# Attention in halves of a query tile: scores of 192 keys on quarter-array tiles, and the older half of the values on two row halves

## Chip, cores, metric

One NeuronCore of a Trainium2 chip runs the whole kernel in one launch. The metric is the device time in microseconds, from the start of the program to its end; lower is better.

## What is computed

One layer (DEPTH is 1) of a hybrid decoder block on x of 2048 tokens by 1024 channels, in float32: an adaptive RMSNorm; one projection to 2048 columns; three mixers side by side (a gated linear recurrence HGRN2 of 4 heads, a causal average pooling of 4 groups, and sliding-window attention); an output projection; a second norm; and a gated MLP of 2816 with a causal convolution of width 3. The change touches the attention:

```python
WINDOW = 128                       # 8 query heads, 2 key/value heads, 64 channels each
s = einsum('bnqhgd,bnkhd->bnhgqk', qb, kb) * 64 ** -0.5   # 128 queries, 256 keys: own and preceding block
rel = qi - kj                                              # query position less key position
in_window = (rel >= 0) & (rel < WINDOW)
s = where(in_window & (blk > 0 or own block), s, -inf)
m = maximum(max(s), sink)
p = exp(s - m); denom = sum(p) + exp(sink - m)
o = einsum('bnhgqk,bnkhd->bnqhgd', p / denom, vb)
```

Each query sees exactly 128 keys: query i of a tile sees keys i+1 to 127 of the preceding tile and keys 0 to i of its own.

## The kernel before

The sequence is worked off in four blocks of 512 tokens. Block 0 is written out on its own (it also splits the weights and computes the modulation), blocks 1 to 3 are one loop body. In a block TensorE (PE) runs 16 units of the input projection (each 8 k-tiles of three matmuls 128x512, because every operand is split in a high and a low part of type fp32r), with the mixers' small matmuls between them, then 8 units of the output projection, then the MLP. The order on every engine is written out by hand; semaphores join them. Plain fp32 matmuls leave two records each in the trace, fp32r ones a single record.

A kv head serves four query heads, so one attention step x_ (0 to 7) is one tile of 128 queries (t = x_ % 4) and one kv head (hh = x_ // 4), four query heads at once. It goes through the engines like this:

- `scores(x_)` on PE: per query head one matmul, 64 channels deep, 128 queries by 256 keys. The two heads of a pair (`par`) lie on the two row halves of the array and write two banks; x_ even uses banks 0 and 1, odd 2 and 3.
- `row_max(x_)` on VectorE (DVE). Since each query sees 128 of the 256 keys, the older key k and the own key k never both count: one `copy_predicated` puts the older scores over those own scores that are masked (mask `older[:, 0]`), and what remains is a row of 128. A `tensor_reduce` for the maximum and two small operations follow.
- `exps(x_)` on ScalarE (ACT): four exponentials with row sums. `normalised(x_)`: DVE makes the reciprocal and scales heads 2 and 3, ACT scales heads 0 and 1.
- `transposed_probs(x_)` on PE (four transposes into bank 4 or 5, by x_ odd or even), `probs_copy(x_)` on ACT copies to PT[.., 1], `masked(x_)` on DVE writes PT[.., 0], the part that belongs to older keys.
- `weighted_values(x_)` on PE into bank 6: all probabilities times the own tile's values VA, plus the masked ones times VD, the older values less the own ones; two heads at a time on the two column halves. `att_high` (ACT) and `att_low` (DVE) split the result for the output projection.

The PE order in this stage: unit 11, two k-tiles of unit 12, `scores(0)`, the last masked product of the recurrence (`level(6)`), `scores(1)`, the rest of unit 12, `recurrence()`, half of unit 13. Then for each x_ from 0 to 7: `scores(x_+2)`, `transposed_probs(x_)`, `weighted_values(x_-1)`, and two to four k-tiles of units 13 to 15 as filler; last `weighted_values(7)`.

The output stage follows at once: `O`, the recurrence's output, is transposed in eight pieces into banks 4 and 5 (line 904), ACT copies each bank into T32 (`to32`, line 1094), DVE splits the copies (`split`, lines 1492 and 1493). PE meanwhile runs `out_unit(0)` and `out_unit(1)` on the attention's channels, then `pooling()` (line 801), whose operand R comes from DVE's `window_sums(0)` and `window_sums(1)` (lines 1584 to 1594), then `out_unit(2)` on the recurrence's channels. DVE's own order there is fixed:

```python
att_low(7)
for a in range(2):
    split(a, a)
window_sums(1)
```

In block 0 only, PE also runs two `gate_rows` (line 592) between `out_unit(1)` and `pooling()`, and GpSimd (POOL) makes the low part of each weight unit (line 514) after ACT has made the high part (line 1003).

`Steps` and `fenced` are ordering helpers: a step waits for its own instruction's semaphore before the next; `fenced` waits and then increments a semaphore of its own.

Of the kernel before, what the change touches and what calls it, by code (L numbers as in the profile page):

```python
# [57 lines left out]
G_BANKS = (4, 5, 4, 5)  # L58
# [39 lines left out]
def hymba_block(nc, x, c, w_ada, b_ada, g_pre_mix, g_post_mix, w_in, hg_norm, pool_w, pool_scale,  # L98
# [19 lines left out]
    with ctx:  # L118
# [23 lines left out]
        VD = sb("VD", [P, TT, P])  # L142
# [55 lines left out]
        mb("A_rest", [P, 1024])  # L198
# [264 lines left out]
        def _(pool):  # L463
# [20 lines left out]
            for q in range(2):  # L484
# [6 lines left out]
                                    pattern=[[-1, P]], channel_multiplier=1))  # L491
            step(pool.memset(negs[:], NEG))
# [38 lines left out]
        def _(pe):  # L531
# [63 lines left out]
            def one_block(b, first):  # L595
# [190 lines left out]
                pe.wait_ge(s["k_copied"], b * 4 + 4)  # L786
# [8 lines left out]
                def pooling():  # L795

                    fenced(s["pool_ready"], b + 1)
                    for a in range(2):
                        for q in range(2):
                            r = slice(64 * q, 64 * q + 64)  # L800
                            ins = mm(ps[r, 6 + a, :], PW[r, a, r], R[r, a, :], start=True, stop=True)
# [29 lines left out]
                def transposed_probs(x_):  # L831
# [3 lines left out]
                    if x_ >= 2:  # L835
                        pe.wait_ge(s["p_copied"], b * 8 + x_ - 1)
                    else:
                        pe.wait_ge(s["hgo_taken"], b * 2 + 2)
                    for n in range(4):
                        ins = tr(ps[:, 4 + x_ % 2, n * P:n * P + P], SM[:, x_ % 3, n, :], ident[:])  # L840
                    ins.then_inc(s["p_tr"], 1)

                def weighted_values(x_):
# [4 lines left out]
                    else:  # L848
                        pe.wait_ge(s["vd_ready"], b + 1)
# [963 lines left out]
```

## Time and profile before

| | |
|---|---|
| runs | 2304.37, 2304.95, 2307.25 us; median 2304.95 |
| profiled execution | 2298.54 us, of which the span from first to last instruction is 2296.8 us |
| granted PE clock | 0.993 of full over the span |
| PE matmuls | 97% of the span |
| VectorE, ScalarE, GpSimd | 53%, 33%, 10% |
| attention's own matmuls | scores 36.3 us, transposes 20.6 us, weighted values 41.1 us of PE busy time |

PE is nearly always occupied, so a matmul's cost is best read as the distance from its start to the start of what follows; the duration of a single record holds the pipeline's depth as well. The three busy times in the last row overlap each other and the work beside them, and so are larger than that distance.

### The profile page before, as it was taken

Reading aid. Unit: us, or ns where it says so; the run is one execution under the profiler, and the core shown is the slowest. Engines: PE = TensorE matmul, PEld = TensorE weight load, DVE = VectorE, ACT = ScalarE, POOL = GpSimd, SP = SyncE. Lnnn points to the kernel's source line nnn. Section 1 sums busy time; section 2 is a strip of 40 time slices with the busy share of each in tenths; the row PEclk is TensorE's granted clock in tenths of the full one; section 3 lists DMA queues with packets and bytes.
Section 4 is the critical chain, followed back from the end, with each engine's and each line's share of the span. In section 5 each row is a group of like instructions: output and inputs, shape, how many; then the busy total and the mean of one; then the engine's idle time right before and its main releaser. Section 6 shows DMA issues by size and latency. Waiting matters only on the chain.

```text
span 2296.8 us, 35674 instructions
## 1 busy us (share of the span) xinstructions
PE 2222.8 (97%) x12603; PEld 1783.1 (78%) x12603; DVE 1215.3 (53%) x2117; ACT 761.6 (33%) x1532; POOL 227.0 (10%) x148
## 2 busy tenths in 40 slices
PE   6999899999999999999999999999999999999997
PEld 4765688788787778888888678888888767888886
DVE  3448484675856655153455755334355665515355
ACT  3545533343444442122134532113024444212212
POOL 2322254444300000000000000000000000000000
PEclk9989999999999999999999999999999999999999
DMA  9963688778573446555554245655546334655555
GB/s 361 367 229 142 226 299 302 278 283 301 189 289 129 148 148 247 192 197 187 192 201 184 103 185 183 238 185 199 188 170 246 129 150 147 244 195 192 192 192 192
DMA packets 115405, 483.29 MB, mean 210 GB/s; under 512 B 7999, under 2 KB 38985, under 8 KB 69705
## 3 DMA queue, kind: packets, MB, share of 16 engines
q1 hardware_dynamic: 115273, 481.53, 57.3%
q8 instruction: 82, 1.34, 0.2%
q14 instruction: 50, 0.41, 0.1%
HBM read 378.74 MB, written 102.76 MB: 210 GB/s over the span
## 4 chain that ended last, share of the span: by engine, by line
PE 88%; DVE 6%; DMA 2%; issue 2%; ACT 1%; SPq 1%; DVEq 0%; POOLq 0%; ACTq 0%
PE ps L609 18%; PE ps L611 18%; PE ps L610 18%; PE ps L634 8%; PE ps L636 8%; PE ps L635 8%; PE ps L734 1%; PE ps L712 1%; PE ps L673 1%; PE ps L853 1%; PE ps L551 1%; DMA AWG<-in_w_ada_dram 1%; PE ps L684 1%; DMA AWT<-in_w_ada_dram 1%; SPq L299 1%
## 5 line engine op out<-in xcount | busy, mean ns | idle before, releaser
L609 PE MATMUL ps<-hTh,wt 128*128 128x512 f32 x1920 | 758.8, 395 | 13.4 <-DVE hTl L1493 9.3
L611 PE MATMUL ps<-hTh,wt 128*128 128x512 f32 x1920 | 748.5, 390 | 0.0
L610 PE MATMUL ps<-hTl,wt 128*128 128x512 f32 x1920 | 748.3, 390 | 0.0
L609 PEld LDWEIGHTS ps<-hTh,wt 128*128 128x128 f32 x1920 | 360.8, 188 | 105.9 <-issue 27.1
L611 PEld LDWEIGHTS ps<-hTh,wt 128*128 128x128 f32 x1920 | 360.8, 188 | 76.3
L610 PEld LDWEIGHTS ps<-hTl,wt 128*128 128x128 f32 x1920 | 361.2, 188 | 71.9
L1736 DVE TENSOR_SCALAR cv<-ub,CW 128x512 f32<-128x512 f32 x176 | 99.9, 567 | 471.4 <-ACT ub L1338 456.5
L1338 ACT ACTIVATE ub<-ps 128x512 f32<-128x512 f32 x176 | 105.5, 599 | 689.5 <-PE ps L611 689.5
L634 PE MATMUL ps<-wt,pTh 128*128 128x512 f32 x704 | 275.0, 391 | 2.2 <-ACT T L1096 2.2
L636 PE MATMUL ps<-wt,pTh 128*128 128x512 f32 x704 | 274.0, 389 | 0.0
L635 PE MATMUL ps<-wt,pTl 128*128 128x512 f32 x704 | 273.9, 389 | 0.0
L514 POOL TENSOR_TENSOR wt<-raw,wt 128x1024 fp32r<-128x1024 f32 x88 | 214.6, 2445 | 399.1 <-ACT wt L1003 399.1
L1738 DVE SCALAR_TENSOR_TENSOR cv<-ub,CW,cv 128x512 f32<-128x512 f32 x176 | 161.6, 918 | 26.8 <-DVE halo L1737 26.8
L1739 DVE SCALAR_TENSOR_TENSOR cv<-ub,CW,cv 128x512 f32<-128x512 f32 x176 | 144.9, 823 | 24.8
L634 PEld LDWEIGHTS ps<-wt,pTh 128*128 128x128 f32 x704 | 132.2, 188 | 29.5 <-issue 2.6
L636 PEld LDWEIGHTS ps<-wt,pTh 128*128 128x128 f32 x704 | 132.1, 188 | 27.5
L635 PEld LDWEIGHTS ps<-wt,pTl 128*128 128x128 f32 x704 | 132.2, 188 | 27.1
L1775 DVE TENSOR_TENSOR Y<-Y,ps 128x512 f32<-128x512 f32 x64 | 43.3, 686 | 172.0 <-PE ps L636 172.0
L1003 ACT ACTIVATE wt<-raw 128x1024 fp32r<-128x1024 f32 x92 | 95.2, 1037 | 60.4 <-PE ps L636 51.2
L1348 ACT ACTIVATE pTh<-P 128x512 f32 (+1 forms) x88 | 55.3, 629 | 154.5 <-DVE P L1745 154.5
L1750 DVE TENSOR_TENSOR pTl<-P,pTh 128x512 f32 x88 | 60.5, 688 | 13.6 <-ACT pTh L1348 13.6
L1745 DVE TENSOR_TENSOR P<-cv 128x512 f32<-128x512 f32 x88 | 65.2, 741 | 3.0
(245 smaller groups left out, 2156.2 us busy)
## 6 DMA issues: line engine op xcount, KB each, us to landing
wt<-split_w SPq DMA_DIRECT2D x268, 1024.0 KB, 4.8
split_w<-wt SPq DMA_DIRECT2D x88, 1024.0 KB, 7.0
raw<-in_w_up_dram SPq DMA_DIRECT2D x22, 1024.0 KB, 9.6
XT<-in_w_ada_dram SPq DMA_DIRECT2D x10, 1024.0 KB, 11.6
XN<-in_x_dram SPq DMA_DIRECT2D x5, 2048.0 KB, 9.9
raw<-in_w_in_dram SPq DMA_DIRECT2D x8, 1024.0 KB, 13.7
XR<-in_x_dram SPq DMA_DIRECT2D x4, 2048.0 KB, 8.0
raw<-in_w_down_dram SPq DMA_DIRECT2D x8, 1024.0 KB, 9.2
```

What stands on the lines that cost most here:

```text
L514: pool.tensor_tensor(lo, src, hi.bitcast(fp32), ALU.subtract).then_inc(s["w_lo"], 1)
L609: mm(ps[:, bank, :], w, hTh[:, k, :], start=(k == 0), stop=False)
L610: mm(ps[:, bank, :], w, hTl[:, k, :], start=False, stop=False)
L611: ins = mm(ps[:, bank, :], wl[:, slot, k, :], hTh[:, k, :], start=False, stop=(k == KD - 1))
L634: mm(ps[:, 4 * n + t, :], h, flat(wh, j), start=f, stop=False)
L635: mm(ps[:, 4 * n + t, :], l, flat(wh, j), start=False, stop=False)
L636: ins = mm(ps[:, 4 * n + t, :], h, flat(wl, j), start=False, stop=e)
L1003: act.activation(hi, src, ACT.Copy).then_inc(s["w_hi"], 1)
L1338: act.activation(ub[:, u, 2:], ps[:, u, :], ACT.Copy).then_inc(s["acc_taken"], 1)
L1736: up(ts(cv[:, u, :], ub[:, u, 2:], tap(2), tap(3), ALU.mult, ALU.add))
L1738: up(stt(cv[:, u, :], ub[:, u, 1:BT + 1], tap(1), cv[:, u, :], ALU.mult, ALU.add))
L1739: stt(cv[:, u, :], ub[:, u, 0:BT], tap(0), cv[:, u, :], ALU.mult, ALU.add)\
```

## The change

- **Scores.** A tile's 128 queries are taken in two halves c of 64. Half c needs only 192 keys, so each head's matmul becomes two of 64 queries by 192 keys; row half by the head (`par`), column half by c. Four such tiles of 64x64 fill the array, 8 matmuls in place of 4. A row's 128 live scores are now in columns 64 to 191. The wait ahead becomes `fenced`.
- **Maximum.** `copy_predicated` covers 4x64 elements per partition in place of 4x128. Where no preceding tile exists (block 0, t = 0), a `tensor_copy` of the constant `negs` is added.
- **Values.** The full probabilities times own values: for half c = 1 with VA as before, for half c = 0 with VS, in which the two 64-token halves are swapped; 4 matmuls of 128 columns. Then the older part: only 64 key positions per half, at 64x64 tiles, with the two halves c on the two row halves and in two banks (5 and 6): 4 matmuls of 128 columns. A `fenced` wait lies between. `masked` is two operations of 64 partitions in place of one of 128. DVE makes VS with two copies per block.
- **Banks.** The attention now writes banks 5 and 6, so that the transposed probabilities have bank 4 alone and each waits for the copy of the one before; pooling writes banks 5 and 6; the recurrence's transposes go to bank 4 and bank 7, and since bank 7 is taken by unit 15, the second four come after `out_unit(0)`.

```diff
                     if x_ >= 2:
-                        pe.wait_ge(s["es_ready"], b * 8 + (x_ - 1))
+                        fenced(s["es_ready"], b * 8 + (x_ - 1))
                     for j in range(2):
-                        for par in range(2):
-                            r = slice(64 * par, 64 * par + 64)
-                            ins = mm(ps[:, 2 * (x_ % 2) + par, j * 256:j * 256 + 256], AQ[r, 2 * hh + j, t * P:t * P + P],
-                                     KT[r, hh, t * P:t * P + 256], start=True, stop=True)
+                        for c in range(2):
+                            for par in range(2):
+                                r = slice(64 * par, 64 * par + 64)
+                                tok0 = t * P + 64 * c
+                                ins = mm(ps[64 * c:64 * c + 64, 2 * (x_ % 2) + par, j * 256:j * 256 + 192],
+                                         AQ[r, 2 * hh + j, tok0:tok0 + 64], KT[r, hh, tok0:tok0 + 192], start=True, stop=True)
...
-                    if x_ >= 2:
-                        pe.wait_ge(s["p_copied"], b * 8 + x_ - 1)
+                    if x_:
+                        pe.wait_ge(s["p_copied"], b * 8 + x_)
...
-                        ins = tr(ps[:, 4 + x_ % 2, n * P:n * P + P], SM[:, x_ % 3, n, :], ident[:])
+                        ins = tr(ps[:, 4, n * P:n * P + P], SM[:, x_ % 3, n, :], ident[:])
...
-                    for g, v in ((1, VA[:, t + 1, hh * 64:hh * 64 + 64]), (0, VD[:, t, hh * 64:hh * 64 + 64])):
-                        pe.wait_ge(s["p_copied" if g else "p_masked"], b * 8 + x_ + 1)
+                    pe.wait_ge(s["p_copied"], b * 8 + x_ + 1)
+                    kv = slice(hh * 64, hh * 64 + 64)
+                    for c in range(2):
                         for par in range(2):
-                            ins = mm(ps[64 * par:64 * par + 64, 6, 0:256], v,
-                                     PT[:, x_ % 2, g, 2 * par:2 * par + 2, :].rearrange("p n q -> p (n q)"),
-                                     start=(g == 1), stop=(g == 0))
+                            mm(ps[64 * par:64 * par + 64, 5 + c, 0:128], VA[:, t + 1, kv] if c else VS[:, t, kv],
+                               PT[:, x_ % 2, 1, 2 * par:2 * par + 2, 64 * c:64 * c + 64], start=True, stop=False)
+                    fenced(s["p_masked"], b * 16 + 2 * x_ + 2)
+                    for c in range(2):
+                        r = slice(64 * c, 64 * c + 64)
+                        for par in range(2):
+                            ins = mm(ps[64 * par:64 * par + 64, 5 + c, 0:128], VD[r, t, kv],
+                                     PT[r, x_ % 2, 0, 2 * par:2 * par + 2, r], start=False, stop=True)
...
-                for a in range(2):
+                def hgrn_channels(a, bank):
                     for t in range(TT):
-                        ins = tr(ps[:, 4 + a, t * P:t * P + P], O[:, t, a * P:a * P + P], ident[:])
+                        ins = tr(ps[:, bank, t * P:t * P + P], O[:, t, a * P:a * P + P], ident[:])
                     ins.then_inc(s["hgt_tr"], 1)
+
+                hgrn_channels(0, 4)
                 pe.wait_ge(s["es_ready"], b * 8 + 8)
                 out_unit(0)
+                pe.wait_ge(s["acc_taken"], eb_ + E_IN)
+                hgrn_channels(1, 7)
                 for u in range(1, U_OUT - 2):
                     if u == 2:
-                        pe.wait_ge(s["acc_taken"], eb_ + E_IN)
                         pooling()
...
-                    step(V.copy_predicated(scores[:, :, 1, :], wide_(older[:, 0, :]).bitcast(i32),
-                                           wide_(negs[:]) if first and t == 0 else scores[:, :, 0, :]))
-                    step(V.tensor_reduce(st[:, 0, v, :], scores[:, :, 1, :], axis=AX, op=ALU.max))
+                    if first and t == 0:
+                        pre_(V.tensor_copy(quarters[0:64, :, 1, :], wide_(negs[0:64])))
+                    step(V.copy_predicated(quarters[:, :, 2, :], wide_(older[:, 0, :]).bitcast(i32),
+                                           wide_(negs[:]) if first and t == 0 else quarters[:, :, 0, :]))
+                    step(V.tensor_reduce(st[:, 0, v, :], rows, axis=AX, op=ALU.max))
...
-                    tt(PT[:, x_ % 2, 0], PT[:, x_ % 2, 1], older[:, 1, :].unsqueeze(1).to_broadcast([P, 4, P]), ALU.mult)\
-                        .then_inc(s["p_masked"], 1)
+                    for c in range(2):
+                        q = slice(64 * c, 64 * c + 64)
+                        tt(PT[q, x_ % 2, 0, :, q], PT[64:128, x_ % 2, 1, :, q],
+                           older[64:128, 1, 0:64].unsqueeze(1).to_broadcast([64, 4, 64]), ALU.mult).then_inc(s["p_masked"], 1)
...
                 tt(VD[:], VA[:, 0:TT, :], VA[:, 1:, :], ALU.subtract).then_inc(s["vd_ready"], 1)
+                V.tensor_copy(VS[0:64], VA[64:128, 0:TT, :]).then_inc(s["vd_ready"], 1)
+                V.tensor_copy(VS[64:128], VA[0:64, 1:, :]).then_inc(s["vd_ready"], 1)
                 row_max(0)
```

PE, the end of the attention and the start of the output stage in the loop body of blocks 1 to 3 (L853 the last weighted values, L904 the transposes of O, L634 to L636 an output unit, L801 pooling). Before, the end of the attention and the first matmuls of `out_unit(0)`:

```order
L853 MATMUL ps<-PT,VA 64x256 [waits p_copied,att_lo]
L853 MATMUL ps<-PT,VA 64x256
L853 MATMUL ps<-PT,VD 64x256 [waits p_masked]
L853 MATMUL ps<-PT,VD 64x256
L904 MATMUL ps<-ident,O 128x128 [waits o_ready,p_copied]
L904 MATMUL ps<-ident,O 128x128 x7
L604 REGISTER_ALU [waits es_ready]
L634 MATMUL ps<-wt,ATT 128x512 [waits att_lo,pair0]
```

Now (L858 and L864 are the weighted values, L914 the transposes, L636 to L638 an output unit, L805 pooling); "..." stands for the rest of `out_unit(0)` and of `out_unit(1)`:

```order
L858 MATMUL ps<-PT,VA 64x128 x2
L864 MATMUL ps<-PT,VD 64x128 [waits p_masked]
L864 MATMUL ps<-PT,VD 64x128 x3
L914 MATMUL ps<-ident,O 128x128 [waits o_ready,p_copied]
L914 MATMUL ps<-ident,O 128x128 x3
...
L636 MATMUL ps<-wt,ATT 128x512 [waits att_lo,pair0]
...
L914 MATMUL ps<-ident,O 128x128 [waits acc_taken]
L914 MATMUL ps<-ident,O 128x128 x3
L636 MATMUL ps<-wt,ATT 128x512 [waits att_lo,pair1]
...
L805 MATMUL ps<-R,PW 64x512 [waits pool_ready]
```

Four of the eight transposes have moved behind the whole of `out_unit(0)`, which is 24 matmuls of 128x512. DVE's order at that place is not touched.

## Rows read from the trace of the kernel before

**Rows 1.** The page's part 1 and part 4: busy time, chain that ended last

```profile
PE 2222.8 (97%) x12603; PEld 1783.1 (78%) x12603; DVE 1215.3 (53%) x2117; ACT 761.6 (33%) x1532; POOL 227.0 (10%) x148
...
PE 88%; DVE 6%; DMA 2%; issue 2%; ACT 1%; SPq 1%; DVEq 0%; POOLq 0%; ACTq 0%
```

**Rows 2.** Timeline of PE, block 1: start us, us, line, operands, count, [idle before <-releaser]

```profile
733.71 1.16 PE L826 MATMUL ps<-SS,QE 64*64 64x64 f32 x64 [0.18 <-PE ps L814]
```

**Rows 3.** Timeline of PE, block 1, step x_ = 1 of the attention

```profile
742.15 1.13 PE L734 MATMUL ps<-KT,AQ 64*128 64x256 f32 x8
743.22 0.66 PE L840 MATMUL ps<-ident,SM 128*128 128x128 f32 x4
743.80 0.65 PE L853 MATMUL ps<-PT,VA 128*64 128x256 f32 x4
744.28 0.60 PE L853 MATMUL ps<-PT,VD 128*64 128x256 f32 x4
744.81 0.50 PE L609 MATMUL ps<-hTh,wt 128*128 128x512 f32 x1
```

**Rows 4.** Timeline of PE, block 1, end of the attention and output stage

```profile
771.81 0.65 PE L853 MATMUL ps<-PT,VA 128*64 128x256 f32 x4 [0.92 <-DVE ATT L1578]
772.41 0.65 PE L853 MATMUL ps<-PT,VD 128*64 128x256 f32 x4
772.99 1.09 PE L904 MATMUL ps<-ident,O 128*128 128x128 f32 x8
773.84 0.48 PE L634 MATMUL ps<-wt,ATT 128*128 128x512 f32 x1
...
784.93 1.93 PE L801 MATMUL ps<-R,PW 64*64 64x512 f32 x8
786.79 0.50 PE L634 MATMUL ps<-wt,hTh 128*128 128x512 f32 x1
```

**Rows 5.** Timeline of DVE, block 1, the same stretch

```profile
762.40 0.69 DVE L1554 COPY_PREDICATED ps<-older,ps 128x512 f32<-128x512 int32 x1
...
767.08 0.68 DVE L1572 TENSOR_TENSOR PT<-PT,older 128x512 f32<-128x512 f32 x1
...
775.84 0.42 DVE L1492 CAST hTh<-T 128x512 fp32r<-128x512 f32 x1
...
782.02 0.18 DVE L1683 TENSOR_SCALAR corr<-ones 128x32 f32<-128x32 f32 x1
```

**Rows 6.** Timeline of ACT, block 1, the same stretch

```profile
763.28 0.39 ACT L1220 ACTIVATE ATT<-ps 128x256 fp32r<-128x256 f32 x1 [0.37 <-PE ps L853]
...
774.05 1.27 ACT L1094 ACTIVATE T<-ps,VT 128x512 f32<-128x512 f32 x2 [0.55 <-PE ps L904]
```

**Rows 7.** Line 1547, DVE: duration ns min/median/max, first and last start

```profile
L1547 DVE COPY_PREDICATED A<-hgmask,ps x48: 421/432/797, 100.8 to 1820.2; 128x256 f32<-128x256 int32 x48
```

**Rows 8.** Timelines of POOL, DVE and PE, block 0, output stage

```profile
219.67 2.80 POOL L514 TENSOR_TENSOR wt<-raw,wt 128x1024 fp32r<-128x1024 f32 x1 [3.83 <-ACT wt L1003]
225.10 2.34 POOL L514 TENSOR_TENSOR wt<-raw,wt 128x1024 fp32r<-128x1024 f32 x1 [2.63 <-ACT wt L1003]
...
220.25 2.77 DVE L1590 TENSOR_TENSOR K<-Q 64x513 f32<-64x513 f32 x1
...
211.85 1.09 PE L904 MATMUL ps<-ident,O 128*128 128x128 f32 x8
...
223.71 1.88 PE L592 MATMUL ps<-AWT,ones 128*128 128x512 f32 x4
225.51 1.93 PE L801 MATMUL ps<-R,PW 64*64 64x512 f32 x8
```

**Rows 9.** Stretches of block 0: us, PE busy (x), PEclk, DMA share, GB/s

```profile
190.00:195.00 5.00, 2.37 (x12) 0.86 0.00 0
195.00:200.00 5.00, 4.84 (x28) 0.80 0.01 3
270.00:280.00 10.00, 5.19 (x20) 1.00 0.25 98
```

More of the change, by code:

```diff
@@ L57 @@
 EVACS = E_UP[2] + U_UP[2]
-G_BANKS = (4, 5, 4, 5)
+G_BANKS = (4, 7, 4, 7)
 ADA_SETS = 6 * D // 512
@@ L141, in hymba_block @@
         negs = sb("negs", [P, P])
-        VD = sb("VD", [P, TT, P])
         cmask = sb("cmask", [P, BT], bf16)
@@ L197, in hymba_block @@
         A = mb("A", [P, TT, HH, CH])
-        mb("A_rest", [P, 1024])
+        VD = mb("VD", [P, TT, P])
+        VS = mb("VS", [P, TT, P])
         VH = mb("VH", [P, TT, 256])
@@ L491, in _ @@
                                     pattern=[[-1, P]], channel_multiplier=1))
+            for i in range(2):
+                step(pool.tensor_copy(older[64:128, i, 0:64], older[64:128, i, 64:128]))
             step(pool.memset(negs[:], NEG))
@@ L785, in one_block @@
                 pe.wait_ge(s["acc_taken"], eb_ + 12)
-                pe.wait_ge(s["k_copied"], b * 4 + 4)
+                fenced(s["k_copied"], b * 4 + 4)
                 scores(0)
@@ L800, in pooling @@
                             r = slice(64 * q, 64 * q + 64)
-                            ins = mm(ps[r, 6 + a, :], PW[r, a, r], R[r, a, :], start=True, stop=True)
+                            ins = mm(ps[r, 5 + a, :], PW[r, a, r], R[r, a, :], start=True, stop=True)
                     ins.then_inc(s["pool_mm"], 1)
@@ L1206, in probs_copy @@
                     act.wait_ge(s["p_tr"], b * 8 + x_ + 1)
-                    act.activation(PT[:, x_ % 2, 1].rearrange("p n q -> p (n q)"), ps[:, 4 + x_ % 2, :], ACT.Copy)\
+                    act.activation(PT[:, x_ % 2, 1].rearrange("p n q -> p (n q)"), ps[:, 4, :], ACT.Copy)\
                        .then_inc(s["p_copied"], 1)
@@ L1219, in att_high @@
                     act.wait_ge(s["pv_mm"], b * 8 + x_ + 1)
-                    act.activation(ATT[:, t, 0, 2 * hh:2 * hh + 2, :],
-                                   ps[:, 6, 0:256].rearrange("p (j q) -> p j q", j=2), ACT.Copy)\
+                    act.activation(ATT[:, t, 0, 2 * hh:2 * hh + 2, :].rearrange("p j (c q) -> p j c q", c=2),
+                                   ps[:, 5:7, 0:128].rearrange("p c (j q) -> p j c q", j=2), ACT.Copy)\
                        .then_inc(s["att_hi"], 1)
@@ L1276, in one_block @@
                     act.wait_ge(s["hgt_tr"], b * 2 + a + 1)
-                    to32(a, ps[:, 4 + a, :], VT[:, 90:91])
+                    to32(a, ps[:, 4 + 3 * a, :], VT[:, 90:91])
                 refill(ub_, OFF_OUT + 4)
@@ L1281, in one_block @@
                 for a in range(2):
-                    to32(2 + a, ps[:, 6 + a, :], VT[:, 80 + a:81 + a])
+                    to32(2 + a, ps[:, 5 + a, :], VT[:, 80 + a:81 + a])
                 if first:
@@ L1550, in row_max @@
                     t, hh, v, k = x_ % 4, x_ // 4, x_ % 3, x_ % 2
-                    scores = ps[:, 2 * k:2 * k + 2, :].rearrange("p a (j g n) -> p (a j) g n", j=2, g=2)
-                    wide_ = lambda y: y.unsqueeze(1).to_broadcast([P, 4, P])
+                    quarters = ps[:, 2 * k:2 * k + 2, :].rearrange("p a (j g n) -> p (a j) g n", j=2, g=4)
+                    rows = ps[:, 2 * k:2 * k + 2, :].rearrange("p a (j n) -> p (a j) n", j=2)[:, :, 64:192]
+                    wide_ = lambda y: y[:, 0:64].unsqueeze(1).to_broadcast([y.shape[0], 4, 64])
                     fenced(s["s_mm"], b * 8 + x_ + 1)
-                    step(V.copy_predicated(scores[:, :, 1, :], wide_(older[:, 0, :]).bitcast(i32),
-                                           wide_(negs[:]) if first and t == 0 else scores[:, :, 0, :]))
-                    step(V.tensor_reduce(st[:, 0, v, :], scores[:, :, 1, :], axis=AX, op=ALU.max))
+                    if first and t == 0:
[3 more added lines that the diff above has]
+                    step(V.tensor_reduce(st[:, 0, v, :], rows, axis=AX, op=ALU.max))
                     step(stt(st[:, 1, v, :], st[:, 0, v, :], -(AD ** -0.5), nsinks[:, hh, :], ALU.mult, ALU.min))
@@ L1577, in att_low @@
                     dve.wait_ge(s["att_hi"], b * 8 + x_ + 1)
-                    tt(ATT[:, t, 1, 2 * hh:2 * hh + 2, :], ps[:, 6, 0:256].rearrange("p (j q) -> p j q", j=2),
-                       ATT[:, t, 0, 2 * hh:2 * hh + 2, :].bitcast(fp32), ALU.subtract).then_inc(s["att_lo"], 1)
+                    halves = lambda i: ATT[:, t, i, 2 * hh:2 * hh + 2, :].rearrange("p j (c q) -> p j c q", c=2)
+                    tt(halves(1), ps[:, 5:7, 0:128].rearrange("p c (j q) -> p j c q", j=2),
+                       halves(0).bitcast(fp32), ALU.subtract).then_inc(s["att_lo"], 1)
                 def window_sums(a):
```

4 lines of the change are left out of this document (2 added, 2 removed).

## The prediction

> **What bounds the kernel now.** I read the page's busy shares first, then its chain of waits, then the timelines of the engines around the change. TensorE (PE) has matmuls under way for 97% of the span and is 88% of the chain that ended last [rows 1]. So time saved on PE is time saved, as long as PE does not stand at a wait that another engine ends. In the attention there is one such wait in each of blocks 1 to 3: the last weighted values stood 0.92 us until DVE had written ATT [rows 4]. I treat these three blocks as one, since they are one loop body with the same order. Times in brackets below are positions in block 1.
>
> **What a pass costs.** The eight transposes of O took 0.85 us (772.99 to 773.84) for eight passes of 128 columns [rows 4]: 0.83 ns a column. An fp32 matmul leaves two records, so two passes. Pooling is eight records on two tiles at a time, four passes of 512 columns: 4 x 0.425 = 1.70 of the 1.86 us from 784.93 to 786.79, which leaves 0.16 us for filling and emptying the array [rows 4]. Scores: four passes of 256, 0.85 of 1.07 us, ends 0.22 [rows 3]. Weighted values: four passes of 256, 0.85 of 1.01 us, ends 0.16 [rows 3]. Four corners really run together: 64 records of 64 columns took 1.16 us [rows 2], that is 16 passes of 0.053 plus 0.3; one after another two by two they would take 1.7.
>
> **The change on PE, step by step.**
> - *Scores.* Sixteen records on four corners are four passes of 192 columns: 0.64 us, plus 0.16 to 0.22 for the ends, so 0.80 to 0.86; I take the middle, 0.83. Saved: 0.24 a step, 1.9 us for a block's eight.
> - *Scores beside level(6).* Both now use 64x64 tiles, so two emptyings of the array go. Each is at most the 0.16 above; I take 0.25 for the two (0 to 0.3).
> - *Values.* The part with all probabilities is four passes of 128, 0.43 + 0.16; the older part two passes of 128, 0.21 + 0.16. Together 0.96 against 1.01. The halved columns nearly all go into the second emptying of the array. Saved: 0.05 a step (bounds: 0.2, if the array need not empty between; a loss of 0.15, if the ends cost what they do at the four-corner row, 0.3 in the second part).
> - *From the fifth values on, PE does not set the pace.* From ACT's copy after weighted_values(4) (763.28) [rows 6] to the last values (771.81) [rows 4] the chain runs through ACT and DVE: exponentials, normalisation, masking, window_sums(0). So only five of the eight value savings count, 0.25 us. In that chain masked(6) becomes two operations. The nearest row for 256 elements is the median 432 ns of line 1547 [rows 7] against 680 ns for the present 512 [rows 5]; issued one after another they cost about 0.1 us more together. The last values then gain 0.2, because what follows their wait (0.58 us, 772.41 to 772.99 [rows 4]) becomes 0.37.
> - *Sum without the moved transposes:* 1.9 + 0.25 + 0.25 - 0.1 + 0.2 = 2.5 us a block.
>
> **On DVE, costed at nothing in blocks 1 to 3.** The masking of the scores halves its elements (0.69 us [rows 5] to about 0.43 [rows 7]). Two copies for VS come ahead of row_max(0), below 0.5 us each by the 0.42 of a cast of 512 elements [rows 5]. Behind them wait row_max(0) and, for PE, the last level's masking; PE has the rest of unit 12 (18 matmuls of 128x512) to run before it needs that. If this cover were gone, up to 0.9 us a block would show. The single bank for transposed probabilities adds a wait for the copy of the step before, made a whole step earlier: nothing.
>
> **The moved transposes: what is late next.** ACT can copy the second half of O only when its transposes are done, and DVE has that half's split ahead of window_sums(1) in its fixed order, on which pooling waits. Count from the first transpose of O, T0 = 772.99. Now PE does four transposes (0.42), out_unit(0) (half of 773.84 to 784.93, 5.5), four more (0.42): T0 + 6.4. ACT starts its copy 0.21 later, as now (773.84 to 774.05), and a copy is half of 1.27 [rows 6], so DVE's second cast comes at T0 + 7.3; before it was at 775.84 [rows 5], T0 + 2.9. From that cast to the end of window_sums(1) DVE needs 6.2 us (775.84 to 782.02 [rows 5]): T0 + 13.5. PE is ready for pooling at T0 + 11.9 as before. **Stall: 1.6 us**, in place of a DVE lead of 2.9 us. Net gain of blocks 1 to 3: 0.9 us each, 2.7 together.
>
> **Block 0.** Its attention stands on DVE for most steps (it computes the gates there), so of PE's 2.5 I count 0.7, which is what DVE's own shorter masking leaves after the VS copies and the constants (0 to 2.5). PE has gate_rows ahead of pooling, which starts at T0 + 13.7 (211.85 to 225.51) [rows 8]: that alone would hide the late sums. But POOL splits weights there. During its 2.80 us operation a DVE operation with two SBUF inputs took 2.77 us [rows 8] where one of 512 elements otherwise takes about 0.7 (0.68 and 0.69 [rows 5]), 2.1 lost. Before, only the first of the two fell into the window sums. Now the first (a little later, since ACT's high part also stands behind the second copy) and the second (225.10, T0 + 13.2) both do: 7.3 + 6.2 + 2 x 2.1 = T0 + 17.7, a stall of 4.0 us. With the 0.7 gained, block 0 loses 3.3.
>
> **Sum.** +3.3 - 2.7 = +0.6 us on the profiled execution's 2298.5, so 2299.1. The median of the runs shown is 6.4 us above that execution, so I forecast 2305.6 us: no difference that can be measured, since this measurement can tell about 0.2%, 4.6 us. Its own range is 2302 to 2309.
>
> **Rivals.**
> - *The stall does not come* (DVE reaches the window sums earlier than I count, or PE later). Then 3 x 2.5 + 0.7 = 8.2 us are gained: 2296.8. For it: the tolerance is small, 1.6 us. Against it: DVE's order in the program, and a delay of 4.4 us against a lead of 2.9. Chance 0.20.
> - *The fences cost PE its overlap (slower).* Seven scores and eight values per block now have a fence. If PE first lets its own matmuls complete there, each costs about the 0.18 us that PE stood at line 826 for its own results [rows 2]. Of them 12 lie ahead of the fifth values: 2.2 us a block, 6.5 in three, about 1 in block 0: 2313. It decides from 0.1 us a fence up. Against it: the level matmuls have such a fence too, and the four-corner row [rows 2] of its kind leaves no room for one per matmul. Chance 0.12.
> - *Weights are not hidden (slower).* With two corners on the same rows, each pass would show its load of 64 columns, about 0.05 us by the ends of scores and pooling (0.22 and 0.16, loads of 128 and 64 columns). Scores would take 1.03, and 1.6 us a block be lost again: 2311. Against it: at [rows 2], with two corners on the same rows as well, 16 passes would then take 1.8 us, not 1.16. Chance 0.07. The Trainium skill (TensorE: Matmul & The Clock Gate, section "Part 3: Packing small matmuls — row/col tiling") states this rule: a weight load overlaps running matmuls only where its row group differs. By that rule the change would hardly pay.
> - *The corners do not do what is said,* two at a time instead of four at 192 columns: scores 1.4 to 1.5 us, 0.4 more than before in place of 0.24 less, 5 us a block: over 2320. No row shows four corners with more than 64 columns. Chance 0.03.
> - *The clock falls in block 0.* PE was busy 2.37 of 5 us from 190 on, and the granted clock fell to its half level for a while (0.86 and 0.80 in two stretches); with 5.19 busy of 10 from 270 on it stayed at 1.00 [rows 9]. A stall of 4 us may do either; the loss at half clock would be about 0.7 + 1.0 us by those two stretches: 2307.3. Chance 0.06.
>
> **How the numbers follow.** Forecast 0.52, the rivals 0.48. Within 0.2%: 0.46 of the forecast, 0.04 of the clock case, 0.50 together. Faster: the missing stall 0.20 and 0.02 of the forecast, 0.22. Slower: 0.12 + 0.07 + 0.03, and 0.04 and 0.02 of forecast and clock case, 0.28. The range runs from 2297 (half of the first rival lies below) to 2313 (half of the fences and all of the serial corners above): some 0.2 outside.
>
> **What would show it.** Scores start 0.8 to 0.9 us before what follows, values 0.95; a wait of pooling for R (line of window_sums) of 1.6 us in blocks 1 to 3 and near 4 us in block 0; the wait of the last values for ATT still about 0.9. Wrong if pooling does not wait, if scores take 1 us or more, or if a new wait stands ahead of scores or between the two parts of the values.

## The result: 0.6% slower, and the profile after

| | median us | range (runs) | to before |
|---|---|---|---|
| before | 2304.66 | 2302.16 to 2307.25 (6) | |
| after | 2317.64 | 2314.19 to 2323.38 (6) | 1.0061 [1.0047, 1.0074] |

I had forecast 2305.6 us and no measurable change; it is 13.0 us slower, beyond the range. The profiled execution of after took 2317.34 us, with a span of 2315.5 us at a granted clock of 0.985.

The page of after, busy shares and chain, against [rows 1]:

```profile
PE 2228.5 (96%) x13115; PEld 1795.1 (78%) x13115; DVE 1220.8 (53%) x2159; ACT 761.1 (33%) x1532; POOL 226.9 (10%) x150
...
PE 86%; DVE 8%; ACT 2%; issue 2%; DMA 1%; SPq 1%; DVEq 0%; ACTq 0%
```

Two points of the chain have gone from PE to DVE. The timeline of PE, a step of the attention in block 1 (start us, us, line, operands, count; against [rows 3]), and from 781 us the end of the attention and the output stage (against [rows 4]):

```profile
753.40 0.88 PE L738 MATMUL ps<-KT,AQ 64*64 64x192 f32 x16
754.21 0.66 PE L844 MATMUL ps<-ident,SM 128*128 128x128 f32 x4
754.80 0.44 PE L858 MATMUL ps<-PT,VS 128*64 128x128 f32 x4
755.07 0.39 PE L858 MATMUL ps<-PT,VA 128*64 128x128 f32 x4
755.38 0.45 PE L864 MATMUL ps<-PT,VD 64*64 64x128 f32 x8
755.76 0.50 PE L611 MATMUL ps<-hTh,wt 128*128 128x512 f32 x1
...
782.12 0.44 PE L858 MATMUL ps<-PT,VS 128*64 128x128 f32 x4 [1.57 <-DVE ATT L1597]
782.38 0.39 PE L858 MATMUL ps<-PT,VA 128*64 128x128 f32 x4
783.11 0.45 PE L864 MATMUL ps<-PT,VD 64*64 64x128 f32 x8 [0.34 <-DVE PT L1590]
783.49 1.11 PE L914 MATMUL ps<-ident,O 128*128 128x128 f32 x4
784.26 0.78 PE L636 MATMUL ps<-wt,ATT 128*128 128x512 f32 x1
...
791.05 0.60 PE L914 MATMUL ps<-ident,O 128*128 128x128 f32 x4
...
800.65 0.50 PE L636 MATMUL ps<-wt,hTh 128*128 128x512 f32 x1
```

Scores start 0.81 us before what follows (754.21 less 753.40), the weighted values 0.96 (755.76 less 754.80): both as costed. At the end the wait for ATT has grown from 0.92 to 1.57 us, and a new one of 0.34 us stands between the two parts of the values. From T0 = 783.49 the second four transposes of O (791.05) start at T0 + 7.6, 1.6 us later than counted (they were to start at T0 + 6.0 and end at T0 + 6.4): the matmul at 784.26 took 0.78 us, since the clock was at its half level there.

The timeline of DVE at the same place, against [rows 5]:

```profile
768.45 0.42 DVE L1570 COPY_PREDICATED ps<-older,ps 128x256 f32<-128x256 int32 x1
...
774.44 0.88 DVE L1590 TENSOR_TENSOR PT<-PT,older 64x256 f32<-64x256 f32 x2
...
785.73 0.43 DVE L1505 CAST hTh<-T 128x512 fp32r<-128x512 f32 x1 [1.26 <-ACT T L1107]
...
792.48 0.43 DVE L1505 CAST hTh<-T 128x512 fp32r<-128x512 f32 x1 [5.60 <-ACT T L1107]
...
798.67 0.18 DVE L1704 TENSOR_SCALAR corr<-ones 128x32 f32<-128x32 f32 x1
```

DVE stood 5.60 us for the second copy of O, and from its cast to the end of the window sums took 6.2 us (792.48 to 798.67), as counted. Only pooling then begins. `masked` is a pair of operations of 0.88 us where one took 0.68.

The list of PE's waits (us in total, times, longest us) has pooling's, of 4.0 us in block 0 and 1.65 in each of the others, and three more that have grown or are new. Before, those for ATT came to 6.3 us, that for SM (block 0, step 4, the normalised probabilities) to 1.6, and the last one was not there:

```profile
PE ps L805 <- DVE R L1613: 8.9, 4, 4.0
...
PE ps L858 <- DVE ATT L1597: 7.5, 6, 1.6
...
PE ps L844 <- ACT SM L1227: 3.2, 1, 3.2
...
PE ps L864 <- DVE PT L1590: 2.0, 6, 0.3
```

And the clock. Stretches of 5 us of after: busy us of PE, PEld, DVE, ACT and POOL, granted clock, DMA share, GB/s; against [rows 9]:

```profile
231.00:236.00 5.00, 4.01 (x9) 1.24 (x10) 1.92 (x7) 0.29 (x1) 0.00 (x0) 0.50 1.03 418
236.00:241.00 5.00, 5.00 (x20) 4.06 (x20) 2.15 (x4) 1.95 (x4) 0.00 (x0) 0.87 0.95 356
...
781.00:786.00 5.00, 3.54 (x24) 2.87 (x25) 2.57 (x6) 1.25 (x3) 0.00 (x0) 0.74 0.67 253
786.00:791.00 5.00, 5.00 (x21) 4.01 (x21) 0.84 (x2) 0.00 (x0) 0.00 (x0) 0.92 0.93 378
836.00:841.00 5.00, 3.60 (x20) 3.60 (x21) 2.10 (x3) 2.30 (x7) 0.00 (x0) 0.71 0.66 249
```

Behind each of three waits, pooling's in block 0 (3.96 us, until 231.99), the one for ATT (1.57 us, until 782.12) and that of the second norm (2.10 us, until 837.40), TensorE ran for some microseconds at 1.2 instead of 2.4 GHz.

### The profile page after: what moved, and what is told of

It reads as the page before. It is cut to its first block, busy times and chain, and to the rows that moved or that the text cites. A ratio compares the mean times of both kernels' runs of the same rounds, so it can differ in the third digit from the quotient of the medians.

```text
span 2315.5 us, 36806 instructions
## 1 busy us (share of the span) xinstructions
PE 2228.5 (96%) x13115; PEld 1795.1 (78%) x13115; DVE 1220.8 (53%) x2159; ACT 761.1 (33%) x1532; POOL 226.9 (10%) x150
## 4 chain that ended last, share of the span: by engine, by line
PE 86%; DVE 8%; ACT 2%; issue 2%; DMA 1%; SPq 1%; DVEq 0%; ACTq 0%
PE ps L611 18%; PE ps L613 18%; PE ps L612 18%; PE ps L636 8%; PE ps L637 8%; PE ps L638 8%; PE ps L714 1%; PE ps L675 1%; PE ps L738 1%; PE ps L553 1%; ACT SM L1211 1%; DMA AWG<-in_w_ada_dram 1%; SPq L299 1%; DMA AWT<-in_w_ada_dram 1%; PE ps L686 1%
## 5 line engine op out<-in xcount | busy, mean ns | idle before, releaser
L636 PE MATMUL ps<-wt,pTh 128*128 128x512 f32 x704 | 275.6, 391 | 2.5 <-ACT T L1109 2.5
L638 PE MATMUL ps<-wt,pTh 128*128 128x512 f32 x704 | 274.7, 390 | 0.0
L636 PEld LDWEIGHTS ps<-wt,pTh 128*128 128x128 f32 x704 | 132.6, 188 | 30.2 <-issue 2.9
L638 PEld LDWEIGHTS ps<-wt,pTh 128*128 128x128 f32 x704 | 132.5, 188 | 27.6
```

The lines of the kernel that those rows point to most:

```text
L636: mm(ps[:, 4 * n + t, :], h, flat(wh, j), start=f, stop=False)
L638: ins = mm(ps[:, 4 * n + t, :], h, flat(wl, j), start=False, stop=e)
```

## The experiments

Twelve kernels. Times of before beside them: 2304.36 us (15 runs) for the first four, 2305.01 (23 runs) for the next four, 2304.30 (33 runs) for the last four.

### Which part costs: the move, undone and alone

`e1_not_moved`, after with the eight transposes of O together again:

```diff
                 hgrn_channels(0, 4)
-                pe.wait_ge(s["es_ready"], b * 8 + 8)
-                out_unit(0)
                 pe.wait_ge(s["acc_taken"], eb_ + E_IN)
                 hgrn_channels(1, 7)
+                pe.wait_ge(s["es_ready"], b * 8 + 8)
+                out_unit(0)
```

> The changed kernel, but the second four transposes of O directly behind the first four again (still into bank 7), so that only their move behind out_unit(0) is undone. Theory (the late window sums make PE wait 1.6 us at pooling in blocks 1 to 3 and 4.0 us in block 0, and these waits bring stretches at half clock, also later ones in the MLP's lead-in): both waits and most of the added half-clock time go, granted clock back to about 0.992, time 2296 to 2300 us. Rival (the waits cost only themselves, 8.9 us, and the clock falls because of something else in the new matmuls, such as the small tiles): 2308 to 2310 us with the clock still near 0.985. Rival (the longer wait for ATT before the last weighted values, 1.6 us in place of 0.9, is the cause): the time stays above 2310.

Measured: 2306.21 us (2302.66 to 2311.59, 11 runs), 1.0008 [0.9998, 1.0018]. The wait of pooling is gone; that for ATT is as in after. The time lies above the theory's range and below both rivals', so none of the three was right as it stood: most of the loss came with the move, but the clock of the profiled execution stayed at 0.986.

`e2_moved_only`, before with the second four transposes behind `out_unit(0)`:

```diff
-                for a in range(2):
+                def hgrn_channels(a):
...
+                hgrn_channels(0)
                 pe.wait_ge(s["es_ready"], b * 8 + 8)
                 out_unit(0)
+                hgrn_channels(1)
```

> The kernel before with one edit: the second four transposes of O (still into bank 5) go behind out_unit(0). Theory: pooling waits 1.6 us in blocks 1 to 3 and about 4 us in block 0, 9 us in all, and half-clock stretches come with them: 2318 to 2328 us, clock about 0.985. Rival (the clock falls from the new small matmuls, not from the waits): 2313 to 2315 us with the clock at 0.993.

Measured: 2319.61 us (2318.03 to 2321.11, 5 runs), 1.0064 [1.005, 1.0078]. The move alone costs more than the whole change. The timeline of PE, block 1, of this kernel:

```profile
785.12 0.66 PE L904 MATMUL ps<-ident,O 128*128 128x128 f32 x4
791.10 0.60 PE L904 MATMUL ps<-ident,O 128*128 128x128 f32 x4
798.79 1.50 PE L801 MATMUL ps<-R,PW 64*64 64x512 f32 x6 [1.60 <-issue]
```

At full clock now, T0 is 785.12, the second four start at T0 + 6.0 (and end at T0 + 6.4), pooling at T0 + 13.7 where before it was T0 + 11.9: the delay forecast, to 0.1 us. (The releaser of this wait is not found by the profile, hence "issue"; in after the same wait is put to R.) The four waits sum to 8.7 us, but the kernel lost 15.3 (the theory's range was 2318 to 2328). Of the rest, 2.3 us are seen in block 0, where the way from pooling to the second norm took 39.7 us in place of 37.4 at a lower clock; against the execution of before in `e12`, some 3.7 us more came behind the second norms, and they were not traced to one cause.

### Whether it is the standing still: the wait filled

`e3_busy_wait`, after with matmuls that nobody reads ahead of pooling, into the bank that pooling then overwrites:

```diff
+                        for i in range(17 if first else 7):
+                            mm(ps[:, 5, :], hTh[:, 7, 0:P], hTh[:, 6, :], start=True, stop=True)
```

> The changed kernel with matmuls 128x512 into a bank nobody reads yet, 7 in blocks 1 to 3 and 17 in block 0, ahead of pooling: PE works through the time in which it would wait (1.6 and 4.0 us), and computes nothing that is used. The time of the waits stays lost. Theory (idle time at this place lowers the clock): the half-clock stretches behind pooling go, the clock rises to about 0.990, and the time falls by 5 to 9 us although work is added: 2308 to 2312. Rival (the clock does not hang on this wait): 2317 to 2319 us, clock 0.985.

Measured: 2313.93 us (2310.39 to 2317.4, 5 runs), 1.0039 [1.0026, 1.0053]. The same stretch of block 0 as above, in this kernel:

```profile
231.00:236.00 5.00, 4.88 (x24) 3.33 (x24) 4.73 (x9) 0.00 (x0) 2.10 (x1) 1.00 1.04 427
236.00:241.00 5.00, 5.00 (x24) 3.48 (x21) 2.33 (x5) 2.25 (x4) 0.00 (x0) 1.00 0.98 327
```

The way from the start of pooling to the second norm is 37.39 us against 39.90: the clock stays at 1.00, and useless work buys 2.5 us. The filler in block 0 is as long as the wait was: from `gate_rows` to pooling PE took 5.90 us here and 5.83 in after (226.16 to 231.99). Pooling comes 1.65 us later than in after, counted from the first transpose of O (215.65 here), because nearly all of that (1.58) was lost ahead of `gate_rows`, where this execution ran at half level behind its wait for ATT and that of after did not:

```profile
229.15 1.88 PE L594 MATMUL ps<-AWT,ones 128*128 128x512 f32 x4
...
235.05 1.93 PE L805 MATMUL ps<-R,PW 64*64 64x512 f32 x8
```

The median is 3.7 us below after's, less than the theory's 5 to 9; as the two intervals overlap, the clock in the rows is the firmer evidence.

### Which waits: DVE's order changed

`e4_sums_later`, after with both window sums moved in DVE's order:

```diff
-                    if x_ == 6:
-                        window_sums(0)
+                window_sums(0)
                 att_low(7)
-                for a in range(2):
-                    split(a, a)
+                split(0, 0)
                 window_sums(1)
+                split(1, 1)
```

> The changed kernel with another order on DVE: split(0), window_sums(1), split(1), and window_sums(0) taken out of step 6 to behind masked(7). The moved transposes stay where the change put them. Theory (all added waits are DVE's order): pooling does not wait, the last weighted values do not wait 1.6 us for ATT either, clock about 0.992: 2290 to 2296 us, below the kernel before by 9 to 14 us. Rival (PE then waits for ATT or the probabilities elsewhere in steps 6 and 7, because ACT's exponentials and DVE's normalisation end last there): 2297 to 2302.

Measured: **2293.70 us** (2291.81 to 2296.4, 5 runs), 0.9956 [0.9943, 0.997]: faster than both kernels, as the theory said, and called the best version below. Its end of the attention in block 1, on PE:

```profile
772.06 0.44 PE L858 MATMUL ps<-PT,VS 128*64 128x128 f32 x4
772.33 0.39 PE L858 MATMUL ps<-PT,VA 128*64 128x128 f32 x4
772.65 0.45 PE L864 MATMUL ps<-PT,VD 64*64 64x128 f32 x8
773.03 0.66 PE L914 MATMUL ps<-ident,O 128*128 128x128 f32 x4
```

No wait stands at the last values, and none at pooling. `window_sums(0)`, 3.6 us, lay in the chain of DVE just where the last values waited.

`e10_pooling_first` takes only the second half of that edit (split, `window_sums(1)`, split), and leaves `window_sums(0)` in step 6.

> Only DVE's order behind the attention is changed (split of the first half, window_sums(1), split of the second); window_sums(0) stays in step 6, and so does the last values' wait for ATT. Theory (waits of pooling 8.9 us, and the half-clock stretch of 3.4 us behind block 0's 4 us wait): 2317.6 less 9 to 13: 2305 to 2309, about the kernel with the transposes unmoved (2306.2), and 11 to 15 us above the kernel with both sums later. Rival (the wait for ATT is a follow-on of the late DVE, and goes too): 2294 to 2299. The wait for ATT should read 1.5 to 1.6 by the theory.

Measured: 2304.99 us (2301.34 to 2309.32, 11 runs), 1.0002 [0.9993, 1.0011]. The theory held: pooling's waits cost 12.7 us (2317.64 less 2304.99), of which 8.9 were waits. Left is the one for ATT, unchanged:

```profile
PE ps L858 <- DVE ATT L1597: 7.5, 6, 1.6
```

The other 11.3 us to the best version come with the place of `window_sums(0)`.

`e9_not_moved_sums_later` has the transposes together as in e1 and `window_sums(0)` behind the loop:

> The unmoved transposes together with window_sums(0) behind the attention: neither the wait of pooling nor the 1.6 us wait of the last values for ATT should be there. Theory (the move itself costs nothing once no engine waits for it, the two waits and the clock behind them are the whole loss): as the kernel with the sums later and the transposes moved, 2293.7, within 2 us, so 2291.5 to 2296. Rival 1 (moving transposes costs time of its own, 0.4 us or more in each block): 2289 to 2291.5. Rival 2 (with the split of O ahead of both window sums, DVE is late for pooling even unmoved, since window_sums(0) now lies there): a wait of pooling of 1 to 2.5 us in each block, 2298 to 2304.

Measured: 2298.96 us (2293.01 to 2301.36, 11 runs), 0.9974 [0.9965, 0.9983]. The median lies in the range of rival 2, but its wait stands in one block only. In blocks 1 to 3 the stages equal the best version's; in block 0 alone pooling waits, by PE's list of waits and DVE's timeline:

```profile
PE ps L805 <- DVE R L1613: 3.2, 1, 3.2
```

```profile
212.72 2.26 DVE L1612 TENSOR_TENSOR K<-K,corr 64x16 f32<-64x16 f32 x1
...
219.22 2.78 DVE L1609 TENSOR_TENSOR K<-Q 128x525 f32<-128x525 f32 x1
...
224.47 2.20 DVE L1612 TENSOR_TENSOR K<-K,corr 64x16 f32<-64x16 f32 x1
```

The last of these is an operation of 16 elements that takes 0.17 us elsewhere; three times in these 15 us a DVE operation with two SBUF inputs took over 2 us, as at the one place in [rows 8]. With the split of the second half behind `window_sums(1)` (e4) DVE is ahead of PE by enough.

`e7_before_sums_later`, before with that one move of `window_sums(0)`:

> The kernel before with one edit: window_sums(0) taken out of step 6 to behind masked(7) on DVE. It takes the wait of 0.9 us for ATT from the last values, in all blocks. Theory (a wait costs itself and, at some phases of the chip's clock control, a stretch at half clock): 3 to 4 us from the waits and up to as much again from the clock: 2297 to 2301 us, clock 0.990 or more. Rival (the sums then make the second window sums late for pooling: DVE needs 3.65 + 0.4 + 2.2 + 5.1 us from the last masking, against 12.5 us of PE): no gain in blocks 1 to 3 and a loss in block 0, 2303 to 2306.

Measured: 2305.97 us (2300.73 to 2310.32, 12 runs), 1.0005 [0.9997, 1.0014], in the rival's range. In blocks 1 to 3 the attention stage shrinks by 1.15 us, as the 0.92 us wait for ATT goes; in block 0 pooling now waits 2.5 us and the clock falls behind it. The move by itself gives nothing.

### The new scores and the new values, each alone

`e5_scores_only` is before with the new `scores`, `row_max`, the columns of `exps` and the fences; `e6_values_only` is e1 with the old ones of these. Both use constant masks that fit one half only, so the probabilities of some older keys differ from the reference's.

> The kernel before with the new scores alone (64x64 tiles, 192 keys, the shorter masking, the fenced waits); the values keep their old form, so half of the queries meet their keys in another order and the attention's output is not the layer's, with the same amounts of work. Theory (matmul times as measured, scores 0.81 to 0.82 us in place of 1.07, and the clock hangs on waits alone): 2 us a block less in blocks 1 to 3, some 0.5 in block 0, no added wait: 2296 to 2299 us with the clock of the kernel before (about 0.989). Rival (the small tiles themselves lower the clock, which is why the kernel without the moved transposes gained nothing): 2303 to 2307 us, clock 0.986 to 0.987.

> The changed kernel without the new scores and with the second four transposes not moved: only the new form of the values, its banks, its copies on DVE and the two masking operations; as above the order of keys does not fit for half of the queries, the amounts of work do. Theory (five of eight value savings of 0.06 us count, 0.3 us a block, and the last values wait somewhat longer for ATT since PE arrives earlier): 2303 to 2305 us, no change. Rival (the values are what brings the half-clock stretches, by the emptying between their two parts or the longer wait for ATT): 2308 to 2312, clock 0.985 to 0.987.

Measured: scores only 2307.69 us (2304.56 to 2312.67, 12 runs), 1.001 [1.0, 1.0021]; values only 2314.14 us (2309.0 to 2317.56, 6 runs), 1.0037 [1.0022, 1.0052]. Both are above what the theories said. For scores only the time comes near the rival's range, but no stretch at half level stands between the first scores and the second norm in its blocks 1 to 3, as it would if the small tiles lowered the clock; both medians are clouded by gaps (8.0 and 4.7 us) that neither before nor after has. Scores only, PE's list of waits and its timeline in block 1:

```profile
PE ps L610 <- issue: 8.0, 5, 2.4
```

```profile
731.75 0.39 PE L612 MATMUL ps<-hTh,wt 128*128 128x512 f32 x1
733.41 0.40 PE L610 MATMUL ps<-hTh,wt 128*128 128x512 f32 x1 [1.27 <-issue]
```

So the way from the first scores to the first transpose of O is compared by stages, without that gap. And values only, the end of its attention:

```profile
774.48 0.44 PE L855 MATMUL ps<-PT,VS 128*64 128x128 f32 x4 [1.64 <-DVE ATT L1591]
774.75 0.39 PE L855 MATMUL ps<-PT,VA 128*64 128x128 f32 x4
775.48 0.45 PE L861 MATMUL ps<-PT,VD 64*64 64x128 f32 x8 [0.34 <-DVE PT L1584]
```

`e11_scores_sums_later` is e5 with `window_sums(0)` behind the loop:

> Before with the new scores alone, and window_sums(0) behind the attention; values, banks and transposes as before (the mask for the older keys does not fit the old values, so those probabilities are not the reference's). Theory (the values' new form earns nothing on the whole: 0.05 us on PE against two masked operations and the VS copies on DVE): without gaps of instruction supply it equals the best version, 2292 to 2295; with the gaps of the scores-only program (about 8 us) 2300 to 2303. Rival (the values' new form is worth its 0.25 to 0.4 us a block): 1 to 2 us above that. A decision needs the stage times: scores(0) to the first transpose of O should be 45.2 by the theory (best version 45.25), 45.6 by the rival.

Measured: 2305.5 us (2303.0 to 2308.72, 11 runs), 1.0009 [1.0, 1.0018], with the same gaps (8.5 us). By the stage the rival held. The stage, in us, blocks 1 to 3, from the start of the first scores to that of the first transpose of O (for after: 736.17 to 783.49); the two kernels with new scores and old values less 1.43 us of gap (1.66 from start to start above, where 0.23 is usual; blocks 1 and 2):

| | old scores, old values | new scores, old values | old scores, new values | both new |
|---|---|---|---|---|
| `window_sums(0)` in step 6 | 49.1 (before) | 46.8 (e5) | 49.7 (e6) | 47.3 (after, e1) |
| behind the loop | 47.9 (e7) | 45.7 (e11) | not run | 45.25 (e4) |

The scores are worth 2.3 us in either row. The values' new form costs 0.5 to 0.6 us where DVE sets the pace of the last steps, and is worth 0.4 where PE does, which is eight times the 0.05 of the prediction. In block 0 scores only took 54.8 us, before 55.4, values only 56.9 and after 56.6.

### The clock at the norm, and before once more

`e8_busy_norm` is e4 with transposes of the identity at the second norm's waits:

```diff
+                    for i in range((0, 4, 18, 0)[t]):
+                        tr(ps[:, 3, t * P:t * P + P], ident[:], ident[:])
```

> The kernel with both window sums later (2293.7 us) and, ahead of the second norm's transposes, where PE waits 0.6 and 2.1 us in every block for DVE, 4 and 18 transposes of the identity into a region that is overwritten afterwards: work that is not used, in time that PE would wait. Theory (idle time ahead of the MLP is what brings the half-clock stretches behind this place): none of them remains behind it in blocks 1 to 3, clock 0.992 or more, 2287 to 2291 us although 88 transposes are added. Rival (transposes do not count as work for the clock control, or the stretches come from elsewhere): clock 0.988, 2293 to 2295 us.

Measured: 2293.25 us (2290.96 to 2295.04, 5 runs), 0.9951 [0.9938, 0.9964], the rival's range: nothing against e4's 2293.70. Two of three half-clock stretches there are missing in the profile, yet the time is the same, so this place offers no gain that can be seen.

`e12_before_again` is the kernel before, unchanged.

> The kernel before once more, unchanged. Theory (the profiled execution on which the prediction rests sat at the top of its range of clocks, 20.5 us at half level where some 40 is usual): a mean clock of 0.987 to 0.991 in the profile, half-clock stretches of 35 to 50 us, and a span of 2301 to 2305 us, with the same waits. Rival (20.5 us is typical and the difference lies elsewhere): clock 0.993 and a span near 2297.

Measured: 2304.45 us (2300.88 to 2307.07, 11 runs), 1.0001 [0.9992, 1.001]. Its profiled execution has a span of 2303.8 us at a granted clock of 0.990. A wait and two stretches:

```profile
PE ps L853 <- DVE ATT L1578: 6.3, 6, 1.3
```

```profile
776.00:781.00 5.00, 4.74 (x28) 3.50 (x29) 2.94 (x7) 1.65 (x3) 0.00 (x0) 1.00 0.89 305
826.00:831.00 5.00, 2.96 (x24) 2.58 (x24) 2.68 (x3) 3.38 (x10) 0.00 (x0) 1.00 0.85 306
```

The theory held. The same waits, but 37 us at the half level where the execution that I read had 20 (the end of the program left out); the 15 runs beside the first four kernels had clocks of 0.987 to 0.992. The profiled execution with its 0.993 was faster by its clock than any of them. In these rows, of block 1, neither the 0.92 us wait for ATT nor, this time, the 2.10 us at the norm brought the half level; behind block 3's norm the same execution had it (granted clock 0.72 from 1920 to 1925 us).

## Why the prediction was wrong, step by step

Against the execution of before that `e12` profiled (and not the one of the prediction, whose clock was higher), after is longer by 11.7 us of span, and by stages (after less before, us):

| from, to | block 0 | blocks 1 to 3 | forecast |
|---|---|---|---|
| first scores, first transpose of O | +1.2 | -1.75, -1.74, -1.71 | -0.7; -2.5 each |
| to pooling | +4.1 | +3.4, +3.4, +1.8 | +4.0; +1.6 each |
| to the second norm | +2.5 | 0.0 each | 0 |
| to the next block or the end | +0.6 | +1.4, -1.0, +0.1 | 0 |

These sum to 12.3, less 0.6 before the first scores. The forecast's sum was +0.6. The missing 11 us are 4.2 in the first row, about 5.9 of clock in the next two (1.7 in each of blocks 1 and 2, 2.5 in block 0), and 0.9 of remainders.

- **Cost of a pass, scores, values.** Right: 0.81 and 0.96 us against 0.83 and 0.96. The emptying between the two parts of the values eats their halved columns.
- **The moved transposes.** Right: 1.6 us forecast and 1.60 to 1.65 measured in blocks 1 to 3, 4.0 and 3.96 in block 0, with POOL's two weight operations both in the window sums. Without this stall (e10) the change comes to no difference from before. The first rival, that it does not come, is out.
- **Masking in two operations.** Mis-sized: I put 0.1 us for the pair in the whole chain, by the 0.42 us row. The pair took 0.88 against 0.68, and the 0.35 us that I counted as the values' gain in the chain became a loss of 0.6 us a block (e6). DVE in block 1, from the masking of step 6 to the window sums, before (the masking itself, 767.08, is in [rows 5]) and then values only:

```profile
767.68 0.17 DVE L1584 TENSOR_SCALAR PV<-PVc 128x16 f32<-128x16 f32 x1
...
769.43 0.87 DVE L1584 TENSOR_TENSOR PT<-PT,older 64x256 f32<-64x256 f32 x2
770.33 0.17 DVE L1597 TENSOR_SCALAR PV<-PVc 128x16 f32<-128x16 f32 x1
```

Counted from the block's first scores (723.92 and 726.19), the window sums start 0.38 us later and the last values 0.40 later, and then the older part waits 0.34 us for the second half of the last masking, so that the first transpose of O is 0.6 late. The savings of the values ahead were real, as PE was 0.27 ahead at the transposes of step 7, but they ended in the wait for ATT, since DVE's chain did not start earlier for them. So the loss is made by the last two maskings and not by every step, and one of my signs of being wrong was there: a new wait between the two parts of the values. With the scores at 2.3 instead of 2.15, this leaves 1.7 of the 2.5.
- **Block 0's 0.7 gained.** The 0.7 was right for scores alone (e5: -0.6). I named DVE as what sets the pace there and then left out its longer masking, and values only is slower by 1.5. Eight times 0.2 would be 1.6, but the timelines do not show it step by step. Counted from the first scores, the transposes of e6 are level with those of before up to step 3 (28.35 and 28.44 us); at step 4 they are 0.9 later, at step 5 1.9, at step 7 1.0, and the end is 1.5 later. At step 4 stands the wait for the normalised probabilities, before and in e6:

```profile
PE ps L840 <- ACT SM L1214: 1.6, 1, 1.6
PE ps L841 <- ACT SM L1224: 2.6, 1, 2.6
```

Behind it e6 ran at half level for longer (granted clock 0.50 from 195 to 200 us, against the 0.80 of [rows 9]). Neither is the cause by itself: e5 has the wait of 2.6 too and was faster than before, and e11, the same program as e5 up to step 6, had more half clock there (0.61 and 0.71 against 1.00 and 0.66 in the two stretches from 190 us) and was only 0.3 later at step 7. How the 1.5 divides stays open; with it, block 0 is at +1.2 instead of -0.7.
- **The clock.** The step that failed most. I gave it 6 chances in 100, in block 0 alone, at 1.7 us. It came in block 0 as that rival says (0.50 for five microseconds, 2.5 us lost), but also behind the waits for ATT, which had grown from 0.92 to 1.6 us (in e6 by 0.4 because DVE ended later and by 0.3 because PE came earlier). I had held against it a stretch in [rows 9] with PE half idle at 1.00; one stretch that stays up is no evidence that another will.
- **The baseline.** Placing the forecast by the median of the runs took care of the lucky execution, but I read the clock's behaviour in blocks 1 to 3 (none lost) off that one execution.
- **Fences.** Not seen: neither scores nor values take longer than I had counted without them.
- **Weights not hidden.** Out: scores would have taken 1.03 us, and took 0.81, with two corners on the same rows. By the rule of the Trainium skill (TensorE: Matmul & The Clock Gate, section "Part 3: Packing small matmuls — row/col tiling"), that a weight load overlaps only where its row group differs, each pass should have shown its load; the trace does not agree.
- **Corners serial.** Out by the same row.

Slower had a chance of 0.28, mostly by mechanisms that did not occur; the one that did, a wait long enough to bring down the clock, was in the list at 0.06 and too small.

## What to carry to other kernels

When work is moved past another unit, count on the consumer's engine what stands behind it in fixed order, and then change that order in the same edit: here two moves on DVE, costing nothing, turn a loss of 0.6% into a gain of 0.4% [0.3, 0.6]. An operation cut in two costs a fixed part twice (0.88 us against 0.68 here), and the place that pays is the engine that sets the pace, not the one for which the cut was made. A stall on a busy TensorE is to be priced at more than its length: here 8.7 to 8.9 us of waits cost 12.7 (e10) and 15.3 (e2).

## What the runs showed of the hardware

**The same wait brings the half clock in one execution and not in another.** The wait for ATT of 1.57 to 1.64 us stands, followed by the 0.34 us one, in 15 places of the profiled executions (after, e1, e3, e6, e10, three blocks each); behind 5 of them the stage up to pooling was longer by the clock. Block 0 has a wait of 1.61 to 1.63 us at the same place in the same five kernels, and the stage behind it was 1.6 us longer in e1, e3, e6 and e10 and not in after: 9 of 20 in all. Behind the 0.9 us wait of before, e2, e5 and e12 this happened in none of 12; without a wait there, in blocks 1 to 3 of e4, e8 and e9, which have the new values too, in none of 9; and behind the 4 us that e3 filled with work not either. What else decides between the nine and the eleven stays open; a run's clock is a matter of some luck, and one profile does not show it.

**Gaps that no engine and no semaphore explains.** In e5 and e11 PE stood 1.0 to 1.6 us between two k-tiles of unit 12, at the same place of the program in each of blocks 1 to 3, and 2.1 to 2.4 us in the input projections of blocks 2 and 3; e6 has two of the latter; before, after, e1 and e4 have none, though their PE instructions at these places are the same. The profile names no releaser ("issue"). That the placing of the program's code plays a part is a guess that wasn't tried. Such a gap can hide a gain: by stages the scores are worth 2.3 us a block, and the median of e5 shows none of it.

**Small DVE operations beside GpSimd.** An operation of 64x16 elements took 2.20 and 2.26 us in block 0 (e9), against 0.17 elsewhere. Both started while a weight operation of GpSimd ran, and ended within 0.03 us of its end (the second at 226.67, GpSimd's at 226.64). It is not only operations with two inputs: in block 0 of after a CAST of one input took 2.21 us in place of 0.43 (from 216.31, GpSimd's from 215.84 to 218.23). So one more instruction in that stretch can cost 2 us.
